# Layer norm of the convolution branch: eight channel tiles added on VectorE, one summed over the partitions on PE

## What is computed

```python
def layer_norm(x, g, b):
    xf = x.astype(jnp.float32)
    mu = jnp.mean(xf, axis=-1, keepdims=True)
    xc = xf - mu
    y = xc * lax.rsqrt(jnp.mean(xc * xc, axis=-1, keepdims=True) + NORM_EPS)
    return (y * g.astype(jnp.float32) + b.astype(jnp.float32)).astype(x.dtype)

def conformer_conv_branch(c, dw_w, dw_b, ln_g, ln_b):
    a, g = jnp.split(c, 2, axis=-1)
    u = a * jax.nn.sigmoid(g)
    u = causal_depthwise_conv(u, dw_w, dw_b)
    u = layer_norm(u, ln_g, ln_b)
    return jax.nn.silu(u)
...
    merged = (g_attn * jnp.einsum("bte,ed->btd", attn, w_o_attn[l])
              + g_rnn * jnp.einsum("bte,ed->btd", rnn, w_o_rnn[l])
              + g_conv * jnp.einsum("bte,ed->btd", cnv, w_o_conv[l]))
    h = h + jnp.einsum("btd,de->bte", merged, w_out[l])
```

## Time and profile before

| | us |
|---|---|
| median of 3 runs | 3741.91 |
| lowest, highest | 3740.64, 3743.09 |
| the profiled execution, its own time | 3738.92 |
| its span in the profile | 3737.1 |

### The profile page before, as it was taken

The page is one execution under the profiler, slowest core; times in us unless marked ns, Lnnn a source line. Parts: engine busy times, 40 slices in busy tenths (PEclk is TensorE's granted clock), DMA queues, the critical chain, the costliest instruction groups (busy, mean ns, idle before and its releaser), DMA issues.

```text
span 3737.1 us, 49849 instructions
## 1 busy us (share of the span) xinstructions
PE 3547.9 (95%) x20100; PEld 3041.0 (81%) x20100; DVE 2446.4 (65%) x2977; ACT 988.4 (26%) x1711; POOL 2058.4 (55%) x1100
## 2 busy tenths in 40 slices
PE   7999898999999999989889999999999999999997
PEld 7898788899999879867677778877887875688886
DVE  6686898777832667679887884378436666653335
ACT  4305542122110340553213111011102444322201
POOL 4355334566666535533455676667665553466664
PEclk9799998999999989989899999999999999999999
DMA  3122111222323312211112343334234442222231
GB/s 136 46 91 74 46 46 57 73 85 92 117 98 100 109 57 80 74 51 46 62 68 85 123 146 105 103 128 139 95 102 156 168 148 76 85 90 95 101 106 69
DMA packets 96898, 348.30 MB, mean 93 GB/s; under 512 B 10848, under 2 KB 13152, under 8 KB 93664
## 3 DMA queue, kind: packets, MB, share of 16 engines
q1 hardware_dynamic: 80064, 289.44, 23.2%
q10 hardware_dynamic: 16672, 56.70, 4.0%
HBM read 322.32 MB, written 23.79 MB: 93 GB/s over the span
## 4 chain that ended last, share of the span: by engine, by line
PE 65%; DVE 24%; ACT 6%; issue 3%; DMA 1%; POOL 0%; ACTq 0%; DVEq 0%; POOLq 0%
PE acc L491 19%; PE acc L492 19%; PE acc L494 19%; DVE cu L2002 10%; PE aux L642 1%; DVE rh L1956 1%; DVE ptmp L2165 1%; PE aux L793 1%; DVE rb L1953 1%; PE acc L822 1%; DVE fpr L1754 1%; DVE sm L1903 1%; DVE mtmp L1808 1%; DVE pcp L2165 1%; ACT L1173 1%
## 5 line engine op out<-in xcount | busy, mean ns | idle before, releaser
L464 POOL TENSOR_SCALAR whi<-raw 128x1024 fp32r<-128x1024 f32 x548 | 630.0, 1150 | 1604.8 <-PE acc L494 1583.7
L466 POOL TENSOR_TENSOR wlo<-raw,whi 128x1024 fp32r<-128x1024 f32 x548 | 1428.6, 2607 | 45.7
L491 PE MATMUL acc<-nhi,whi 128*128 128x512 f32 (+1 forms) x2776 | 955.3, 353 | 49.6 <-DVE mt L2011 22.4
L492 PE MATMUL acc<-nlo,whi 128*128 128x512 f32 (+1 forms) x2776 | 945.9, 349 | 0.0
L494 PE MATMUL acc<-nhi,wlo 128*128 128x512 f32 (+1 forms) x2776 | 867.3, 348 | 0.0
L491 PEld LDWEIGHTS acc<-nhi,whi 128*128 128x128 f32 x2776 | 526.0, 189 | 138.1 <-issue 47.0
L491 PE MATMUL acc<-bhi,whi 128*128 128x264 f32 (+1 forms) x1864 | 557.9, 315 | 39.1 <-DVE merged L2071 13.2
L492 PEld LDWEIGHTS acc<-nlo,whi 128*128 128x128 f32 x2776 | 525.4, 189 | 69.1
L492 PE MATMUL acc<-blo,whi 128*128 128x264 f32 (+1 forms) x1864 | 547.1, 310 | 0.0
L494 PEld LDWEIGHTS acc<-nhi,wlo 128*128 128x128 f32 x2776 | 486.5, 190 | 67.9
L2002 DVE SCALAR_TENSOR_TENSOR cu<-cx,par,cu 128x528 f32<-128x528 f32 (+1 forms) x480 | 490.6, 1083 | 0.0
(11 more groups left out here) (365 smaller groups left out, 4509.0 us busy)
## 6 DMA issues: line engine op xcount, KB each, us to landing
raw<-in_w SPq DMA_DIRECT2D x548, 512.0 KB, 3.3
kept_cp<-pcp ACTq DMA_DIRECT2D x4, 1280.0 KB, 6.6
cp<-kept_cp ACTq DMA_DIRECT2D x4, 1280.0 KB, 10.3
kept_ap<-pap ACTq DMA_DIRECT2D x4, 1024.0 KB, 4.0
kept_cs<-pcs ACTq DMA_DIRECT2D x4, 1024.0 KB, 6.5
ap__143<-kept_ap ACTq DMA_DIRECT2D x4, 1024.0 KB, 6.7
cs__154<-kept_cs ACTq DMA_DIRECT2D x4, 1024.0 KB, 6.6
merge_gates<-gout ACTq DMA_DIRECT2D x16, 256.0 KB, 2.9
```

Source lines behind the costliest of these rows:

```text
L464: pool.tensor_scalar(hi, w, 1.0, 0.0, ALU.mult, ALU.add).then_inc(sem("w_hi"), 1)
L466: pool.tensor_tensor(lo, w, hi.bitcast(F32), ALU.subtract).then_inc(sem("w_split"), 1)
L491: pe.matmul(acc[s][:, f, 0:TH], hi, xh[:, f * TH:(f + 1) * TH], start=a, stop=False)
L492: pe.matmul(acc[s][:, f, 0:TH], hi, xl[:, f * TH:(f + 1) * TH], start=False, stop=False)
```

## The change

The 8 tiles are added element by element on DVE into one tile, and PE sums that tile over the partitions with one matmul for each half of the columns. This is done for the values (row 2 of `cstat`, free until the reciprocal) and for the squares (row 1).

- PE: `ln_mean` and `ln_square` each call `column_sums`, which waits until all 8 tiles have been added and runs 2 matmuls instead of 16. Their places among the gate tiles stay.
- DVE, values: 7 additions a layer. Five stand in the loop of merged tiles, behind the taps of m = 0, 1, 2, 4 and 5 (SUMMED_AT gives the tile), two behind the last tap.
- DVE, squares: 7 additions a layer, each behind the centring of a later tile. ACT's square of tile n now waits for DVE's addition of tile n - 2 in place of PE's sum of it, since `csq` has two slots.
- ACT: the two waits for the sums go by another semaphore. Its instructions stay.
- The two loads of the attention gates count on one semaphore, and every sigmoid waits for both.

```diff
+SUMMED_AT = {0: 1, 1: 2, 2: 3, 4: 4, 5: 5}
...
+            def column_sums(l, dst, src, ready):
+                pe.wait_ge(sem(ready), (l + 1) * KD)
+                W = LT[l] // 2
+                for f in range(2):
+                    m = pe.matmul(dst[:, f, 0:W], ones[:, :], cstat[:, src, f * W:(f + 1) * W], start=True, stop=True)
+                m.then_inc(sem("cv_column_sums"), 1)
...
             def ln_mean(l):
-                for n in range(KD):
-                    pe.wait_ge(sem("cv_conv"), (l * 8 + n // 2 * 2 + 2) * DW)
-                    if n == 0:
-                        pe.wait_ge(sem("at_scored"), AT_FROM[l + 1])
-                    W = LT[l] // 2
-                    for f in range(2):
-                        m = pe.matmul(aux[0][:, f, 0:W], ones[:, :], cu[:, n, LO[l] + f * W:LO[l] + (f + 1) * W],
-                                      start=n == 0, stop=n == KD - 1)
-                m.then_inc(sem("cv_mean"), 1)
+                pe.wait_ge(sem("at_scored"), AT_FROM[l + 1])
+                column_sums(l, aux[0], 2, "cv_added")
             def ln_square(l):
-                for n in range(KD):
-                    pe.wait_ge(sem("cv_square"), l * 8 + n + 1)
...
-                    m.then_inc(sem("cv_summed"), 1)
+                column_sums(l, aux[1], 1, "cv_summed")
...
-                            act.dma_start(sga[:, n:n + 4], gates[HEADS + n:HEADS + n + 4].rearrange("a p n -> p a n"))                               .then_inc(sem(f"att_gates_back{n // 4}"), 16)
+                            act.dma_start(sga[:, n:n + 4], gates[HEADS + n:HEADS + n + 4].rearrange("a p n -> p a n"))                               .then_inc(sem("att_gates_back"), 16)
...
             def mg_att(l, taps):
+                def added(n):
+                    if n % 2 == 0 or n == 1:
+                        dve.wait_ge(sem("cv_conv"), (l * 8 + n // 2 * 2 + 2) * DW)
+                    if n == 1:
+                        dve.wait_ge(sem("at_p"), AT_FROM[l + 1])
+                        dve.wait_ge(sem("at_turned"), AT_FROM[l + 1])
+                        dve.tensor_tensor(cstat[:, 2, 0:T], cu[:, 0, o:], cu[:, 1, o:], ALU.add).then_inc(sem("cv_added"), 2)
+                        return
+                    dve.wait_ge(sem("cv_added"), l * KD + n)
+                    dve.tensor_tensor(cstat[:, 2, 0:T], cstat[:, 2, 0:T], cu[:, n, o:], ALU.add).then_inc(sem("cv_added"), 1)
...
                     for _ in range(TAPS_MERGE):
                         next(taps, None)
+                    if m in SUMMED_AT:
+                        added(SUMMED_AT[m])
                 for _ in taps:
                     pass
+                added(6)
+                added(7)
...
                 dve.wait_ge(sem("cv_mean_read"), l + 1)
                 for n in range(KD):
+                    centred(n)
+                    if n >= 3:
+                        squares_added(n - 2)
+                squares_added(6)
+                squares_added(7)
                 dve.wait_ge(sem("cv_std"), l + 1)
```

More of the change, by code:

```diff
@@ L2025, in mg_att, with centred, squares_added @@
                         next(taps, None)
+                    if m in SUMMED_AT:
+                        added(SUMMED_AT[m])
                 for _ in taps:
                     pass
+                added(6)
+                added(7)
+                def centred(n):
+                    dve.tensor_tensor(cu[:, n, o:], cu[:, n, o:], cstat[:, 0, 0:T], ALU.subtract).then_inc(sem("cv_centred"), 1)
+                def squares_added(n):
+                    dve.wait_ge(sem("cv_square"), l * 8 + n + 1)
+                    if n == 1:
+                        dve.tensor_tensor(cstat[:, 1, 0:T], csq[:, 0, 0:T], csq[:, 1, 0:T], ALU.add).then_inc(sem("cv_summed"), 2)
+                        return
+                    dve.wait_ge(sem("cv_summed"), l * 8 + n)
+                    dve.tensor_tensor(cstat[:, 1, 0:T], cstat[:, 1, 0:T], csq[:, n % 2, 0:T], ALU.add).then_inc(sem("cv_summed"), 1)
                 dve.wait_ge(sem("cv_mean_read"), l + 1)
                 for n in range(KD):
-                    dve.tensor_tensor(cu[:, n, o:], cu[:, n, o:], cstat[:, 0, 0:T], ALU.subtract).then_inc(sem("cv_centred"), 1)
+                    centred(n)
[3 more added lines that the diff above has]
+                squares_added(7)
                 dve.wait_ge(sem("cv_std"), l + 1)
```

10 lines of the change are left out of this document (3 added, 7 removed).

## The result

| | before | after |
|---|---|---|
| median, us | 3742.44 (4 runs, 3740.64 to 3743.09) | 3766.72 (4 runs, 3758.46 to 3767.61) |
| ratio to before | | 1.0063 [1.005, 1.0075] |
| the profiled execution, us | 3738.92 | 3766.41 |
| its span, us | 3737.1 | 3764.6 |
| mean granted clock of TensorE | 0.972 | 0.964 |

The account below looks back on a forecast made before the run. DVE was taken to bound the merge loop, and PE's instruction order the time behind it in layer 0. Terms 5.5 + 2.4 + 7.0 + 8.0 = 22.9 us on 3741.9 gave 3764.8; range 3752 to 3775, its own 3760 to 3770.

Parts of the forecast that it names:

- The mean path: Last taps to the mean's sum: 1.3 us late plus 2.4 for a split in layer 0, 4.2 in layer 1.
- Point 1: Merge loop: some 3.5 us more on DVE from first to last merged tile, with five adds of 0.7 between.
- The last tap: End of the convolution taps: the forecast would be wrong if the last tap came no later than before.
- The split in the tail: POOL's weight split falling on the adds behind the taps: 2.4 us in layer 0, nothing added in layer 1.
- Point 2: PE's wait list: the single sums wait for cstat four times, some 35 us in all.
- Point 4: First add of squares takes over 2 us; fourth gate tile's end to fifth's start 12 to 14 instead of 8.8.
- The meeting: First add of squares starting inside POOL's subtraction: 2.0 us more.
- Point 3: Behind PE's four waits the granted clock is near 0.5 to 0.6: 2.0 us lost each, 8.0 in all.
- Point 5: Later stages: the out, up and down tiles are all shifted by the same amount.
- The clock didn't stay up: Rival: PE's granted clock doesn't fall in the new waits, 8.0 us goes, 3756.8; chance 0.12.
- The loop's adds weren't hidden: Rival: order of taps, splits and tiles absorbs the merge loop's adds, 7.0 us goes, 3757.8; chance 0.12.
- The faster case: Rival: DVE holds POOL's splits off more often in the loops, each saving 2.4 us; 12 give 3736.0; chance 0.03.

Follow-up runs that it names:

- values_only: Changed kernel's adds for the mean only, PE summing the squares of eight tiles as in the kernel before: 3750.11 us, ratio 1.0025.
- split_later: Changed kernel, with POOL's split freed by the fourth gate tile's end held until DVE has added the squares: 3762.4 us, ratio 1.0059.
- kept_warm_24: Changed kernel, with PE making 24 short unread sums while it waits for the squares: 3760.05 us, ratio 1.005.
- kept_warm: Changed kernel, with PE making 18 short unread sums while it waits for the squares: 3762.56 us, ratio 1.0053.
- the two halves: Against the kernel before, only the values added on DVE (3750.11 us), or only the squares added on DVE (3746.87 us).
- split_behind_taps: Changed kernel, with POOL's split freed by the second gate tile's end held until DVE has added the values: 3760.21 us, ratio 1.0048.
- early_sums: Kernel before, with PE summing tiles 0 to 5 for the mean ahead of the second gate tile, 6 and 7 ahead of the third: 3735.3 us, ratio 0.9986.
- gate_in_wait: Changed kernel, with PE making the fifth gate tile before the sum of the squares: 3765.93 us, ratio 1.0068.

## Why the prediction was right, and where it wasn't

The forecast was 22.9 us over the profiled execution; the layers show 22.1, and the executions 27.5, the medians of one comparison 24.3. The mechanism in the layers was the forecast one. That the median also came within 2 us is in part luck: outside the layers the profiled executions of these kernels lie between 4 us under before and 7 over it, for which the forecast had no term, and inside them some errors cancel. By its steps:

- **The mean path** (1.3 + 2.4 in layer 0, 4.2 in layer 1, without the clock). ACT's copy of the mean comes 5.6 and 4.3 us later. Some 0.7 of each is the single sum at the low clock, which stood under the clock. That leaves 4.9 against 3.7, and 3.6 against 4.2. In layer 1's other arrangement (values_only) it would be 5.7.
- **Point 1, the last merged tile +3.5,** came out in no trace. In layer 0 it is +0.15 (103.79 against 103.64) or +2.4, in layer 1 +5.1 (106.41 against 101.35) or +1.8, by the arrangement of the loop. DVE's adds do lengthen its queue, but they move it against POOL's, and which instructions pay for a split changes. In layer 0 of after the bill came in the last 11 taps (+7.9), which the prediction had put at one split; in layer 1 those taps became 5.0 us cheaper. Over the layer the price was right: 3.8 and 4.6 us with the adds alone, against 3.5.
- **The last tap.** In layer 1 of after it comes no later than before (115.1 against 115.2 us), which the prediction had named as a sign that it is wrong. The adds were paid for all the same, through the last merged tile and the two adds behind the taps.
- **The split in the tail.** Predicted 2.4 for layer 0 and nothing for layer 1, on the ground that layer 1's last taps carry a split already. Holding it off brought the mean 2.9 us forward in both, so layer 0's term was rightly counted and layer 1's was missing.
- **Point 2, four waits of some 35 us:** 33.9. The parts at the mean were wrong and cancel: 7.5 us in layer 0 against 4 to 6, and 4.6 in layer 1 against 9, since PE reached its sum 114.9 us behind the first merged tile and not at the 111.2 of the forecast.
- **Point 4, the squares:** the first add takes 2.31 and 2.34 us. From the end of the fourth gate tile (755.09 - 11.00 = 744.09) to the fifth's start at 756.64 it is 12.55 us instead of 8.8, within the 12 to 14 predicted; 1989.81 - 10.81 = 1979.00 to 1991.33 is 12.3 in layer 1. Without the clock's 1.35 and 1.8 the gates lie 3.0 us further apart in each layer, where 3.5 was forecast. The meeting is worth 1.6, by split_later, and not 2.0.
- **Point 3, the clock:** 8.75 us lost against 8.0, with the granted clock at 0.50 behind each wait. kept_warm_24 took the two restarts at the squares away and found 1.35 and 1.8 us. Counted at the gates, all four come to 7.5 us rather than 8.75 (0.7 in each single sum for the mean, 1.4 and 1.6 up to the fourth gate, and these two).
- **Point 5, all later tiles late by the same amount:** nearly. 1.7 us came between the stretches and 3.1 behind layer 1. No experiment ties these to the change: kept_warm, whose layers are as long as the changed kernel's, has a median 4.2 us lower, and the two halves gain there where the whole loses. What moves this rest wasn't settled. DVE and POOL meet in most phases, and a shift changes which instructions do; this is argued, not shown.

Of the rivals none came true. The clock didn't stay up. The loop's adds weren't hidden. The faster case, POOL held off more often, was not seen in either layer's total: in layer 1 the 86 taps became cheaper, 92.5 us instead of 102.6, but the adds took 9.2 (7.7 + 1.5) instead of 7 x 0.69 = 4.8, and smaller instructions grew (the additions to `merged` from 6.3 to 8.9, the first taps of a tile from 1.0 to 3.7). The groups of DVE between the layer's first merged tile and the end of its tail (of after, 1844.7 to 1964.1 us; before, 1831 to 1949, the taps were `x86 | 102.6, 1263`):

```profile
L1998 DVE SCALAR_TENSOR_TENSOR cu<-cx,par,cu 128x512 f32<-128x512 f32 x86 | 92.5, 1146 | 0.0
...
L2023 DVE TENSOR_TENSOR cstat<-cstat,cu 128x512 f32<-128x512 f32 x6 | 7.7, 1280 | 0.1
...
L2020 DVE TENSOR_TENSOR cstat<-cu 128x512 f32<-128x512 f32 x1 | 1.5, 1518 | 0.0
```

## What to carry to other kernels

Taking matmuls from PE pays only where PE is last; here 6.1 us less of them, four times, became 33.9 us of waiting, because DVE's adds stood on the path and PE's ended in its shadow. Before replacing sums by adds on another engine, ask which inputs are ready early and sum those where PE has to pass anyway: that won 2.9 us a layer without a single new instruction, though in layer 1 only because a split then missed the taps. And a wait of PE can cost more than its length: behind each of the four here the clock was low for 2.9 to 5.5 us. Last, two traces of kernels that share their instructions can differ by 1 to 3 us in one stretch. Before a difference of that size is put down to an edit, look for a third trace in which the stretch ran the same way.

## What the runs showed of the hardware

- After 8.17 us of float32 sums and 3.00 us of standing (kept_warm), PE came back at 0.51 of its clock; after 24 sums instead of 18 and 0.33 us of standing, at 1.00.
- The time for which the clock stays low behind a restart differs even between traces of the same instructions. It was 2.9 to 5.5 us among the four restarts of the changed kernel. In the loop, behind the same wait ending at the same time of the layer, it was 2.8 or 4.6 us in layer 0 and 3.1 or 6.0 in layer 1, and the kernels' loops fall into two arrangements by it. Coming back 1.6 us sooner (split_later) gave half of that away in layer 0 and nothing in layer 1.
- What a split costs DVE depends on where it falls: 1.6 us at the first add of squares, 2.9 in the tail. It went away where the split fell into DVE's idle time (split_later), was held behind the adds (split_behind_taps) or fell behind the last tap by itself (early_sums). Part of the gain was lost again where the clock then stayed low for longer.
- The end of a tile on PE starts a split on POOL. So moving a tile of PE forward can slow DVE, as in gate_in_wait, where a tile put into a wait made the wait's chain 3.1 us longer, with one centring at 2.85 us instead of 0.70.
